# Query transposes taken in the second chunk, and the first attention scores written ahead of the last chunk's outputs

## The reference

```python
# the delta rule, one direction; a chunk is a tile of tokens
decay = exp(where(incl, gc[:, None] - gc[None, :], -inf))
a_mat = eye + where(strict, (k * beta) @ k.T * decay, 0)
u, wk = solve_triangular(a_mat, [v * beta, k * beta * exp(gc)])
qk    = (q @ k.T) * decay
def step(S, chunk):
    v_new = u - wk @ S
    o     = (q * exp(gc)) @ S + qk @ v_new
    S     = S * exp(gc[-1]) + k_dec.T @ v_new

# the attention of the latent tokens over themselves (with a bias) and the context
s = concat([q @ k.T + bias, q @ kc.T])
o = softmax(s) @ concat([v, vc])
```

## Time and profile before

| | us |
|---|---|
| median of 3 runs | 1728.99 |
| lowest, highest | 1726.43, 1731.76 |
| profiled execution, in all | 1725.56 |
| its span, first to last instruction | 1723.8 |
| PE busy | 1670.2 (97%) |
| DVE busy | 1064.1 (62%) |
| ACT busy | 844.9 (49%) |
| POOL busy | 53.3 (3%) |

### The profile page before, as it was taken

The page is one execution under the profiler, slowest core; times in us unless marked ns, Lnnn a source line. Parts: engine busy times, 40 slices in busy tenths (PEclk is TensorE's granted clock), DMA queues, the critical chain, the costliest instruction groups (busy, mean ns, idle before and its releaser), DMA issues.

```text
span 1723.8 us, 24263 instructions
## 1 busy us (share of the span) xinstructions
PE 1670.2 (97%) x9904; PEld 1359.4 (79%) x9904; DVE 1064.1 (62%) x1590; ACT 844.9 (49%) x1244; POOL 53.3 (3%) x54
## 2 busy tenths in 40 slices
PE   8999998999999999999999999999999999999998
PEld 2778887886688887888888888788878878888886
DVE  3589676754665456645876555655565557865554
ACT  3454477654444344645555444444335546454442
POOL 0000134100000000000000000000000000000000
PEclk9999999999999999999999999999999999999999
DMA  8333431012475555544455555655555434455553
GB/s 357 129 122 116 157 113 27 14 65 79 159 284 177 193 190 179 195 144 136 157 214 181 191 189 180 237 185 181 195 180 192 169 123 167 171 214 178 194 179 115
DMA packets 41519, 285.72 MB, mean 166 GB/s; under 512 B 4417, under 2 KB 6593, under 8 KB 8001
## 3 DMA queue, kind: packets, MB, share of 16 engines
q1 hardware_dynamic: 39120, 268.61, 44.2%
q0 software_dynamic: 2288, 15.56, 2.3%
HBM read 283.11 MB, written 1.05 MB: 165 GB/s over the span
## 4 chain that ended last, share of the span: by engine, by line
PE 88%; DVE 5%; ACT 3%; issue 2%; DMA 2%; SPq 0%; POOL 0%; DVEq 0%; ACTq 0%; POOLq 0%
PE psum L430 85%; PE psum L433 3%; DMA ring<-stream 1%; DVE ring_lo L1891 1%; DVE arena L1885 1%; DMA arena<-stream 1%; ACT w_hi L1415 1%; ACT arena L1415 0%; DVE arena L2367 0%; ACT L1706 0%; ACT cst L1415 0%; DVE sblk L1957 0%; DVE cst L1891 0%; DVE cst L1885 0%; DVE psum L1888 0%
## 5 line engine op out<-in xcount | busy, mean ns | idle before, releaser
L1891 DVE TENSOR_TENSOR ring_lo<-ring,w_hi 128x1024 fp32r<-128x1024 f32 x416 | 489.2, 1221 | 239.5 <-ACT w_hi L1415 237.8
L1415 ACT ACTIVATE w_hi<-ring 128x1024 fp32r<-128x1024 f32 x416 | 415.5, 1052 | 291.6 <-DMA ring<-stream 227.1
L430 PE MATMUL psum<-w_hi,xT_hi 128*128 128x512 f32 (+1 forms) x1184 | 465.0, 393 | 10.4 <-DVE xT_lo L1891 9.7
L430 PE MATMUL psum<-w_hi,xT_lo 128*128 128x512 f32 (+1 forms) x1184 | 459.6, 388 | 0.0
L430 PE MATMUL psum<-ring_lo,xT_hi 128*128 128x512 f32 (+1 forms) x1184 | 459.1, 388 | 0.0
L430 PEld LDWEIGHTS psum<-w_hi,xT_hi 128*128 128x128 f32 x1184 | 223.6, 189 | 56.1 <-issue 12.1
L430 PEld LDWEIGHTS psum<-w_hi,xT_lo 128*128 128x128 f32 x1184 | 223.4, 189 | 46.3
L430 PEld LDWEIGHTS psum<-ring_lo,xT_hi 128*128 128x128 f32 x1184 | 223.9, 189 | 43.6
L1885 DVE TENSOR_TENSOR arena<-psum,arena 128x256 f32<-128x256 f32 (+1 forms) x144 | 73.6, 519 | 149.1 <-ACT arena L1717 123.5
L1415 ACT ACTIVATE arena<-psum 128x512 f32<-128x512 f32 (+6 forms) x161 | 84.9, 555 | 146.8 <-PE psum L430 120.2
L430 PE MATMUL psum<-w_hi,hfT_hi 128*128 128x512 f32 x352 | 137.7, 391 | 0.0
(11 more groups left out here) (256 smaller groups left out, 1822.0 us busy)
## 6 DMA issues: line engine op xcount, KB each, us to landing
ring<-stream SPq DMA_DIRECT2D x249, 1024.0 KB, 4.8
arena<-ln_params POOLq DMA_DIRECT2D x6, 1024.0 KB, 5.8
arena<-par POOLq DMA_DIRECT2D x2, 1858.0 KB, 10.2
arena<-stream SPq DMA_DIRECT2D x3, 1024.0 KB, 6.9
arena<-x_in POOLq DMA_DIRECT2D x2, 1024.0 KB, 9.2
ring<-rpb_bands SPq DMA_DIRECT2D x4, 512.0 KB, 6.1
cst<-const POOLq DMA_DIRECT2D x1, 1728.0 KB, 7.5
arena<-ctx_in POOLq DMA_DIRECT2D x1, 1024.0 KB, 19.2
```

Source lines behind the costliest of these rows:

```text
L430: owe(nc.tensor.matmul(o, lhsT, rhs, start=first, stop=last), sem)
L1415: return A(o, i, ACT.Copy)
L1891: return V_.tensor_tensor(o, a, b, ALU.subtract)
```

## The change

On PE, `queries()` moves from the first chunk (behind the last step of gate block 3) to the second, behind `scaled_keys(3)`. On ACT the two copies to `dqT` move with it, from behind `gate_block(3)` and ahead of the wait for `zeros`, to behind the `kbT` copies of the second chunk. At the end of the delta rule, `values(3)` moves behind PE's waits for `nakT` and `naqT`, and `chunk_outputs(3)` moves behind `na_scores(0)`. The orders of DVE, GpSimd and SyncE stay as they are.

```diff
@@ PE, first chunk
             steps(6, KD)
-            queries()
             last_level_in(0)
@@ PE, second to fourth chunk
                 if n == 1:
                     decays(3, 1, 1)
                     scaled_keys(3)
+                    queries()
                 elif n == 2:
                     attention_keys((3,))
...
                 if n == 2:
                     state_queries(2)
-            values(3)
-            chunk_outputs(3)
-
             def na_scores(i):
...
             for t in range(4):
                 moved(pe, ("nakT", t))
             for t in range(2):
                 moved(pe, ("naqT", t))
+            values(3)
             na_scores(0)
+            chunk_outputs(3)
             for i in range(16):
@@ ACT
                 if n == 0:
                     second_level_to_64(n)
                     gate_block(3)
-                    for t in range(2):
-                        evacuate(("dqT", t), dqT[:, :, t * P:(t + 1) * P], by128)
                     act.wait_ge(S("zeros"), 2)
...
                 if n < 2:
                     scaled_keys(n + 2)
+                if n == 1:
+                    for t in range(2):
+                        evacuate(("dqT", t), dqT[:, :, t * P:(t + 1) * P], by128)
                 elif n == 3:
```

## The result

The changed kernel takes 1737.38 us (median of 9 runs, 1732.21 to 1743.69), the kernel before 1728.99 us in the same comparison (9 runs, 1721.33 to 1731.76). The ratio is 1.0054, 95% interval 1.0038 to 1.0070: slower by half a per cent, some 9 us, where I had forecast +3.0 us and a range that ended at 1736. The profiled execution of the changed kernel took 1737.38 us, its span 1735.6 us, against 1723.8 before: 11.8 us more.

The account below looks back on a forecast made before the run. PE was taken to bound the kernel; 0 + 0.87 + 1.53 + 1.0 - 0.36 gave +3.0 us on the 1728.99 median, 1732.0 us, with as many clock falls as before (chance 0.57). Range: 1727.5 to 1736 us.

Parts of the forecast that it names:

- What bounds the kernel: Whole span: PE, busy 97%; a delay between 267 and 400 us moves the end by as much.
- (a): First chunk: removing the queries gains 0, since ACT's diagonal(0) still waits for GpSimd's clearing until 274.01.
- Rival 1: First chunk: ACT starts diagonal(0) at 272.74 after all, gaining 1.30 us; sum +1.7, 1730.7 us; chance 0.08.
- The hole ahead of `last_level_out(0)`: First chunk, PE idle until 278.78: grows from 1.99 to about 2.6 us.
- (b): Second chunk, PE: eight query transposes ahead of state_keys(1) cost +0.87 us; the two ACT copies are hidden.
- (c): Last chunk, PE: values(3) waits for the last naqT copy and starts at about 368.17 instead of 366.64, +1.53 us.
- (d): Last chunk: scores ahead of outputs delay DVE's outputs by 1.0 us; 0.36 comes back from its wait for scores.
- The hole ahead of `na_probs(0)`: Start of the softmax, PE idle: grows from 1.29 to 1.9 us.
- The clock: 379 to 397 us: a 3.4 us stretch at half clock costs at most 1.7 us; forecast assumed as many falls as before.
- rival 2: Longer holes ahead of values(3) and na_probs(0) each bring one more 1.7 us clock fall: 1733.7 or 1735.4 us; chance 0.22.
- The sign that I had named: Changed profile: the forecast would be wrong if the number of stretches at 1.2 GHz changed.
- The rule of the Trainium skill: Three lengthened PE gaps: its advice against long idle gaps speaks against the change; by it, two more falls, +6.4 us.

Follow-up runs that it names:

- e1_queries_only: Kernel before, with only the queries and their copies moved to the second chunk, the end of the last chunk unchanged: ratio 1.0000.
- e9_same_work_behind: Changed kernel plus seven 128x128 matmuls of constants behind the waits for nakT and naqT, ahead of values(3): ratio 1.0020 to the kernel before.
- e3_no_wait_hole: Kernel before, with only na_scores(0) moved ahead of chunk_outputs(3) on PE; values(3) stays ahead of the waits, queries in the first chunk: ratio 1.0006.
- e5_hole_filled: Changed kernel plus seven 128x128 matmuls of constants ahead of the waits for nakT and naqT, filling the hole: ratio 1.0012 to the kernel before.
- e6_hole_half_filled: Changed kernel plus three 128x128 matmuls of constants ahead of the waits for nakT and naqT: ratio 1.0017 to the kernel before.
- e10_twice_behind: Changed kernel plus fourteen 128x128 matmuls of constants behind the waits for nakT and naqT, ahead of values(3): ratio 1.0025 to the kernel before.

## Why the prediction was wrong, point by point

- **What bounds the kernel, and the engine that is late in each chunk.** Right. What was lost at 365 to 405 us was still there at the end: the first matmuls of 128x512 in the attention start at 392.95 before and at 404.66 with the change, and from there to the end of the span it is 1330.8 and 1330.9 us.

```profile
392.95 3.63 PE L430 MATMUL psum<-arena,cst 128*128 128x512 f32 x4 [1.78 <-ACT arena L1682]
...
404.66 1.96 PE L430 MATMUL psum<-arena,cst 128*128 128x512 f32 x4 [0.83 <-ACT arena L1682]
```

- **(a) The first chunk gives nothing.** Right, and by the mechanism named: the clearing on GpSimd covers the two copies. Rival 1 did not happen. The hole ahead of `last_level_out(0)` was 2.48 us, about 2.6 was said.
- **(b) Queries in the second chunk, 0.87.** Right in the trace to the digit (1.74 for sixteen transposes); alone, `e1_queries_only` is not to be told from nothing. The copies were hidden: ACT waited 1.44 us for PE behind them.
- **(c) The wait ahead of `values(3)`, 1.53.** The mechanism was right, its direct price was too small by half a microsecond. From the first of the eight transposes to `values(3)` it was 0.95 us before and is 366.65 - 363.66 = 2.99 now, so 2.04. The copy ended at 364.99 + 1.09 = 366.08 and PE began 0.57 later, where I had allowed 0.05. In `e9_same_work_behind`, where matmuls of constants stand directly behind the waits, PE began at 369.38, 0.25 behind the copy's end (368.05 + 1.08). The other 0.32 thus lie with `values(3)` itself, probably with its own waits, which PE's sequencer had worked off beside other work before; that was not measured apart. ACT in the changed kernel and in `e9_same_work_behind`:

```profile
364.99 1.09 ACT L1414 ACTIVATE arena<-psum 128x512 f32<-128x512 f32 x2
...
368.05 1.08 ACT L1419 ACTIVATE arena<-psum 128x512 f32<-128x512 f32 x2
```

- **(d) Scores ahead of the outputs.** Right in kind: 1.20 measured in `e3_no_wait_hole` where 1.0 was said, net 0.84 where 0.64 was said.
- **The hole ahead of `na_probs(0)`, 1.9.** 1.79 in `e5_hole_filled`, `e6_hole_half_filled`, `e9_same_work_behind` and `e10_twice_behind`, where the clock had held until then; 0.85 in the changed kernel, where PE itself was slow.
- **The clock. Here is the step that failed.** I priced a fall at 1.7 us, "a stretch of 3.4 us at half the clock costs at most half of itself", because every fall near it in the kernel before lasted 3.4 us. The fall behind the new hole lasted 34.1 us. Between the start of `values(3)` and the first scores the changed kernel needs 382.98 - 366.65 = 16.33 us, before 8.52, `e3_no_wait_hole` 9.36: some 7 us of the loss arise in these few steps. Another 3.9 us arise in the first steps of the softmax, at the same low clock: up to the 128x512 matmuls above it is 404.66 - 382.98 = 21.68 us, against 392.95 - 375.16 = 17.79 before. So rival 2 was the right mechanism in the right place with the price of one fall, and I gave it 0.22. I looked at the length of holes only, and set against the rival that 2.2 us with 0.21 busy had passed without a fall. What stands behind a hole was not in the argument. The earlier trace rows had one side of it, 64 records of 64 columns among the 80; the other was not among the rows: behind the hole of the earlier trace rows the narrow records (64x64) last only 1.1 us, and from 279.86 on comes work of 512 and 128 columns. The sign that I had named, another number of stretches at 1.2 GHz, did not come either: each of the two traces has nine in the whole span, and it is the length of one that changed.
- **The rule of the Trainium skill** ("TensorE: Matmul & The Clock Gate", section "Why this matters for your kernels": no long idle gaps of TensorE between bursts of matmuls) spoke against the change, and the result agrees with its direction. By the length that the section gives, though, none of the three gaps would have counted as long, so my appeal to it was loose. As a rule of length it does not sort these runs: behind 1.90 us the clock stayed low for 34.1 us, behind 2.48 us for 3.4 us.
- **The range** ended at 1736.0, the price of two short falls. With one of 34 us, worth up to 17, it would have had to reach beyond 1740; the runs reach to 1743.69.

## What to carry to other kernels

Before a wait is moved ahead of a block of work on TensorE, see what the block is made of: a hole of under 2 us in front of a long run of narrow float32 matmuls cost three times the hole and the reorder together (some 9 us against 2.04 + 0.84), while wide matmuls directly behind it, or no hole, kept the clock. Let the wait stand behind the work that doesn't need it, as the kernel before did with `values(3)`. And when one engine's order is changed so that a result is ready earlier, change the order of the engine that takes it too: the scores ahead of the outputs were no gain on PE alone (0.84 us later in the trace, ratio 1.0006, not to be told from nothing) and 4.3 us on PE and DVE.

## What the runs showed of the hardware that I had not expected

- At 1.2 GHz TensorE stayed for 34.1, 27.3, 30.7, 17.1 and 13.7 us in five profiled executions with the hole and the narrow work, while its records say it was busy for over 95% of the stretch. Busy time in the records was thus no sign that the full clock would come back. What ends such a stretch stays open: it ended some 2 us into a run of wider matmuls in two kernels, and without one in three. A single group of scores, eight records of 256 columns, stood in the fall of the kernel before that ended after 3.4 us (379.4 to 382.8); four such groups stood in the 34.1 us of the changed kernel, from 373.1, 382.1, 388.7 and 395.8 on, and it went on behind each.
- The same 80 records take 9.3 to 9.6 us at the full clock and 15.8 to 18.1 us when the clock falls at their start or shortly ahead of it.
- Seven matmuls of constants, 1.7 us of work whose result is thrown away, made the changed kernel some 7 us faster.
- Two engines can hide the same delay at the same moment: the two copies on ACT ended at 274.02 and the clearing on GpSimd at 274.01, so that taking the copies away changed nothing (`e1_queries_only`, ratio 1.0000).
